# The first sixteen modulation units computed from rounded parts, in a fused two-block transformer kernel on one core

## The reference, cut to what matters

```python
c_act, cc_act = silu(c), silu(c_ctx)              # 1024 numbers each
mod   = c_act  @ ada_w[l] + ada_b[l]              # 1024 x 6144 for each layer l
mod_c = cc_act @ ada_w[l] + ada_b[l]
sh1, sc1, g1, sh2, sc2, g2 = split(mod, 6)
h  = x   * (1 + sc1)  + sh1                       # nothing else can start before this
hc = ctx * (1 + csc1) + csh1
```

## Time and profile before

| what | value |
|---|---|
| median of 3 runs | 2089.61 us (2089.19 to 2090.86) |
| the profiled execution | 2090.49 us, of which the span of its instructions is 2088.7 us |
| busy share of TensorE, VectorE, ScalarE, GpSimd | 93%, 58%, 44%, 52% |
| mean granted TensorE clock over the span | 0.966 of 2.4 GHz |
| HBM read | 342.68 MB, 165 GB/s over the span |
| first projection matmul starts | 46.41 us after the span's start |

### The profile page before, as it was taken

The page is one execution under the profiler, slowest core; times in us unless marked ns, Lnnn a source line. Parts: engine busy times, 40 slices in busy tenths (PEclk is TensorE's granted clock), DMA queues, the critical chain, the costliest instruction groups (busy, mean ns, idle before and its releaser), DMA issues.

```text
span 2088.7 us, 32983 instructions
## 1 busy us (share of the span) xinstructions
PE 1947.9 (93%) x11578; PEld 1617.5 (77%) x11578; DVE 1201.9 (58%) x2445; ACT 928.5 (44%) x1441; POOL 1082.7 (52%) x451
## 2 busy tenths in 40 slices
PE   7999888789979889969998989999999999999998
PEld 2644343589969779959777769999999998888887
DVE  1122645364455465450365231999999986777776
ACT  2212555445444445445524244654444445445553
POOL 0434556554439554427734047887666664444443
PEclk9998889799999999989999999999999999999999
DMA  8535465445545445535422335554444445555554
GB/s 288 172 131 171 151 217 181 139 159 182 190 141 181 159 150 185 189 112 195 162 88 83 120 121 179 184 181 152 145 150 147 147 148 191 194 192 191 192 194 156
DMA packets 95134, 345.08 MB, mean 165 GB/s; under 512 B 10512, under 2 KB 11840, under 8 KB 94528
## 3 DMA queue, kind: packets, MB, share of 16 engines
q1 hardware_dynamic: 90720, 329.82, 47.8%
q10 hardware_dynamic: 4320, 13.97, 2.0%
HBM read 342.68 MB, written 1.06 MB: 165 GB/s over the span
## 4 chain that ended last, share of the span: by engine, by line
PE 52%; issue 16%; DVE 14%; POOL 12%; DMA 3%; ACT 2%; ACTq 0%; POOLq 0%; SPq 0%; DVEq 0%
PE ps L505 18%; PE ps L458 16%; POOL ring_lo L403 10%; PE ps L442 4%; PE ps L649 3%; DMA ring<-stream 3%; PE ps L574 2%; PE ps L758 2%; DVE hot_hi_a L2279 1%; PE ps L720 1%; DVE hot_hi_b L2279 1%; DVE hot_lo_b L2280 1%; DVE hot_lo_a L2280 1%; DVE arena L1624 1%; DVE arena L2290 1%
## 5 line engine op out<-in xcount | busy, mean ns | idle before, releaser
L403 POOL TENSOR_TENSOR ring_lo<-ring,ring_hi 128x1024 fp32r<-128x1024 f32 x435 | 1047.2, 2412 | 993.5 <-ACT ring_hi L397 992.7
L397 ACT ACTIVATE ring_hi<-ring 128x1024 fp32r<-128x1024 f32 x580 | 613.4, 1058 | 573.3 <-DMA ring<-stream 570.1
L458 PE MATMUL ps<-h_lo,ring_hi 128*128 128x256 f32 x2096 | 295.9, 284 | 0.0
L458 PEld LDWEIGHTS ps<-h_lo,ring_hi 128*128 128x128 f32 x2096 | 272.2, 193 | 0.0
L505 PE MATMUL ps<-ring_hi,e_pair 128*128 128x512 f32 x1024 | 255.9, 391 | 2.6 <-DVE e_pair L2314 2.2
L2314 DVE TENSOR_TENSOR e_pair<-arena,e_pair 128x256 fp32r<-128x256 f32 x128 | 174.5, 1363 | 99.1 <-ACT e_pair L1477 99.1
L505 PEld LDWEIGHTS ps<-ring_hi,e_pair 128*128 128x128 f32 x1024 | 193.0, 189 | 43.8 <-DVE e_pair L2314 3.0
L403 DVE TENSOR_TENSOR ring_lo<-ring,ring_hi 128x1024 fp32r<-128x1024 f32 x145 | 191.9, 1324 | 5.0 <-ACT ring_hi L397 3.2
L505 PE MATMUL ps<-ring_hi,arena_r 128*128 128x512 f32 x704 | 186.2, 399 | 1.2 <-ACT ring_hi L397 1.2
L458 PE MATMUL ps<-late_r,ring_hi 128*128 128x256 f32 x1136 | 162.6, 286 | 0.0
L1980 DVE CAST arena_r<-arena 128x256 fp32r<-128x256 f32 x64 | 62.3, 974 | 169.5 <-ACT arena L1359 169.5
(11 more groups left out here) (278 smaller groups left out, 2463.1 us busy)
## 6 DMA issues: line engine op xcount, KB each, us to landing
ring<-stream SPq DMA_DIRECT2D x628, 512.0 KB, 3.3
arena<-ln_rows ACTq DMA_DIRECT2D x8, 512.0 KB, 5.8
arena<-ada_rows ACTq DMA_DIRECT2D x4, 512.0 KB, 4.6
arena<-decay ACTq DMA_DIRECT2D x1, 1536.0 KB, 7.2
cst<-consts ACTq DMA_DIRECT2D x1, 1036.0 KB
h<-x_t ACTq DMA_DIRECT2D x1, 1024.0 KB
arena<-ctx_t ACTq DMA_DIRECT2D x1, 1024.0 KB
late<-bias_rows ACTq DMA_DIRECT2D x1, 1024.0 KB, 7.9
```

Of the source, the lines that this page charges most:

```text
L397: act.activation(ring_hi[:, s, :], ring[:, s, :], ACT.Copy).then_inc(hi_ready, 1)
L403: eng.tensor_tensor(ring_lo[:, s, :], ring[:, s, :], ring_hi[:, s, :], ALU.subtract).then_inc(lo_ready[s], 1)
L458: m = pe.matmul(ps[:, bank, 0:T], w[:, kc * P:(kc + 1) * P], x[:, kc, :], start=begin, stop=w is w_lo and kc == KC - 1)
```

## The change

Units 0 to 15 are split like all later modulation units. Their products are made with `cact4` (the rounded and the remaining part of silu(c), four columns) instead of `cact`: two products with the rounded unit and two with the rest. ScalarE rounds each of the sixteen units; DVE subtracts for the even ones and POOL for the odd ones. ScalarE issues only the parameters first. The constants and the four small inputs are issued behind the rounding of unit 0 (`consts_in`, `rows_in`), the tokens behind that of unit 4, the context behind that of unit 6 (`inputs`, now counted to 2). ScalarE copies row g out behind the rounding of the last unit of row g+1, and the exp of the two lambda sums moves behind the sixteen roundings. On DVE the lambda work moves behind the first four subtractions. `bias_row` goes through bank 2 instead of 7 and stands before the last `early_columns`; DVE works on its result before the last `mod_columns`. POOL's eight subtractions stand in front of those of the later units.

```diff
-SPLIT_STAGES = (*(f"ada_mid{_n}" ...
+SPLIT_STAGES = ("ada0", *(f"ada_mid{_n}" ...
-                one(7, relb[0:32, 0:8], oneh[0:32, :], ps[0:8, 7, 0:DIST])
+                one(2, relb[0:32, 0:8], oneh[0:32, :], ps[0:8, 2, 0:DIST])
-            pe.wait_ge(cact_ready, 1)
+            pe.wait_ge(cact4_ready, 1)
             def early_rows(g):
-                    w = unit(FIRST_UNIT["ada0"] + 4 * g + k4)
-                    for k2 in range(2):
-                        kc = 2 * k4 + k2
-                        m = pe.matmul(ps[0:2, b, :], cact[:, kc, :], w[:, k2 * 512:(k2 + 1) * 512],
+                    u = FIRST_UNIT["ada0"] + 4 * g + k4
+                    w_hi, w_lo = split_unit(u)
+                    for w in (w_hi, w_lo):
+                        if w is w_lo:
+                            wait_unit_lo(u)
+                        for k2 in range(2):
+                            kc = 2 * k4 + k2
+                            m = pe.matmul(ps[0:4, b, :], cact4[:, kc, :], w[:, k2 * 512:(k2 + 1) * 512],
...
             for g in range(EARLY_ADA // 4):
                 early_rows(g)
                 if g == 0:
-                    pe.wait_ge(inputs, 16 * 7)
+                    pe.wait_ge(consts_in, 16)
                 else:
                     early_columns(g - 1)
+            pe.wait_ge(rows_in, 16 * 4)
+            bias_row()
             early_columns(EARLY_ADA // 4 - 1)
-            bias_row()
...
# ScalarE
-            for dst, src in ((relb[0:32, :], rel_bias), ..., (cst[:, :], consts), (h[:, :, :], x_t), (z, ctx_t)):
-                act.dma_start(dst, src).then_inc(inputs, 16)
...
+            for k in range(EARLY_ADA):
+                unit_hi(act, FIRST_UNIT["ada0"] + k)
+                if k == 0:
+                    act.dma_start(cst[:, :], consts).then_inc(consts_in, 16)
+                    for dst, src in ((relb[0:32, :], rel_bias), (oneh[0:32, :], onehot), (dmask[0:8, :], dist_mask),
+                                     (lamb, lam_in)):
+                        act.dma_start(dst, src).then_inc(rows_in, 16)
+                if k == 4:
+                    act.dma_start(h[:, :, :], x_t).then_inc(inputs, 16)
+                if k == 6:
+                    act.dma_start(z, ctx_t).then_inc(inputs, 16)
+                if k % 4 == 3 and k > 4:
+                    early_row_out(k // 4 - 1)
+            act.wait_ge(lam_sum, 1)
+            act.activation(lam2, lam2, ACT.Exp).then_inc(act_step, 1)
+            early_row_out(EARLY_ADA // 4 - 1)
# VectorE
+            dve.wait_ge(cact_hi, 1)
+            dve.tensor_tensor(cact4[:, :, 2:4], cact[:, :, :], cact4[:, :, 0:2], ALU.subtract).then_inc(cact4_ready, 1)
+            for k in range(0, 8, 2):
+                unit_lo(dve, FIRST_UNIT["ada0"] + k)
+            dve.wait_ge(rows_in, 16 * 4)
...
             for g in range(EARLY_ADA // 4):
+                if g < 2:
+                    for k in (8 + 4 * g, 10 + 4 * g):
+                        unit_lo(dve, FIRST_UNIT["ada0"] + k)
+                if g == 3:
+                    filled(2)
+                    step(dve.tensor_copy(rowbuf[0:8, :], ps[0:8, 2, 0:DIST]))
...
                 mod_columns(0, 6 + g % 2, 4 * g)
# GpSimd
+            for k in range(1, EARLY_ADA, 2):
+                unit_lo(pool, FIRST_UNIT["ada0"] + k)
```

More of the change, by code:

```diff
@@ L86 @@
 PROJ_UNIT = [FIRST_UNIT[f"proj{_n}"] for _n in range(N_PROJ)]
-SPLIT_STAGES = (*(f"ada_mid{_n}" for _n in range(N_PROJ)), "ada_late", "attn_out", "mlp0", "conv_in", "conv_out", "mlp1",
+SPLIT_STAGES = ("ada0", *(f"ada_mid{_n}" for _n in range(N_PROJ)), "ada_late", "attn_out", "mlp0", "conv_in", "conv_out", "mlp1",
                 "in2_qk", "in2_v", "in2_gates", "out2", "peer_q", "peer_u", "peer_v")
@@ L333, in build @@
         params_in = sem("params_in")
+        consts_in = sem("consts_in")
+        rows_in = sem("rows_in")
         inputs = sem("inputs")
@@ L587, in early_rows @@
                 for k4 in range(4):
-                    w = unit(FIRST_UNIT["ada0"] + 4 * g + k4)
-                    for k2 in range(2):
-                        kc = 2 * k4 + k2
-                        m = pe.matmul(ps[0:2, b, :], cact[:, kc, :], w[:, k2 * 512:(k2 + 1) * 512],
-                                      start=kc == 0, stop=kc == KC - 1)
-                        if k2 == 0:
-                            m.then_inc(units_begun, 1)
+                    u = FIRST_UNIT["ada0"] + 4 * g + k4
[6 more added lines that the diff above has]
+                            m = pe.matmul(ps[0:4, b, :], cact4[:, kc, :], w[:, k2 * 512:(k2 + 1) * 512],
+                                          start=w is w_hi and kc == 0, stop=w is w_lo and kc == KC - 1)
+                            if w is w_hi and k2 == 0:
+                                m.then_inc(units_begun, 1)
                 m.then_inc(full[b], 1)
@@ L603, in early_columns @@
                 for q in range(4):
-                    m = pe.matmul(ps[:, b, 2 * q:2 * q + 2], early_row[0:2, g, q * P:(q + 1) * P],
-                                  const("ident")[0:2, 0:2], start=True, stop=True)
+                    m = pe.matmul(ps[:, b, 2 * q:2 * q + 2], early_row[0:4, g, q * P:(q + 1) * P],
+                                  const("pair", 2)[0:4, :], start=True, stop=True)
                 m.then_inc(full[b], 1)
@@ L795, in _ @@
             pe.wait_ge(h_act, 1)
-            pe.wait_ge(cact4_ready, 1)
             projections()
@@ L1136, in _ @@
             act.dma_start(par[:, :], params).then_inc(params_in, 16)
-            for dst, src in ((relb[0:32, :], rel_bias), (oneh[0:32, :], onehot), (dmask[0:8, :], dist_mask),
-                             (lamb, lam_in), (cst[:, :], consts), (h[:, :, :], x_t), (z, ctx_t)):
-                act.dma_start(dst, src).then_inc(inputs, 16)
             act.wait_ge(params_in, 16)
@@ L1144, in _ @@
             act.activation(cact4[:, :, 0:2], cact[:, :, :], ACT.Copy).then_inc(cact_hi, 1)
-            act.wait_ge(lam_sum, 1)
-            act.activation(lam2, lam2, ACT.Exp).then_inc(act_step, 1)
             def drain(b, dst, func=ACT.Copy, n=T, **kw):
@@ L1150, in drain, with early_row_out @@
                 act.activation(dst, ps[:, b, 0:n], func, **kw).then_inc(emptied[b], 1)
-            for g in range(EARLY_ADA // 4):
+            def early_row_out(g):
                 act.wait_ge(full[EARLY_BANKS[g]], 1)
-                act.activation(early_row[0:2, g, :], ps[0:2, EARLY_BANKS[g], :], ACT.Copy).then_inc(
+                act.activation(early_row[0:4, g, :], ps[0:4, EARLY_BANKS[g], :], ACT.Copy).then_inc(
                     emptied[EARLY_BANKS[g]], 1)
+            for k in range(EARLY_ADA):
[14 more added lines that the diff above has]
+            early_row_out(EARLY_ADA // 4 - 1)
             drains[4].add()
@@ L1169, in _ @@
             act.wait_ge(mod_cols, 1)
+            act.wait_ge(inputs, 16 * 2)
             for c, src in enumerate((h, z)):
@@ L1526, in _ @@
             n_rstd = Count()
-            dve.wait_ge(params_in, 16)
-            dve.wait_ge(inputs, 16 * 7)
+            dve.wait_ge(cact_hi, 1)
[3 more added lines that the diff above has]
+            dve.wait_ge(rows_in, 16 * 4)
             step(dve.tensor_tensor(lamw, lamb[:, 0:4:2, :], lamb[:, 1:4:2, :], ALU.mult))
@@ L1536, in _ @@
             step(dve.tensor_scalar(mqg, param("mq_g"), SCALE, None, ALU.mult))
[L1537 to L1543, removed]
             def mod_columns(l, bank, at):
@@ L1552, in _ @@
             for g in range(EARLY_ADA // 4):
-                mod_columns(0, 6 + g % 2, 4 * g)
+                if g < 2:
[4 more added lines that the diff above has]
+                    step(dve.tensor_copy(rowbuf[0:8, :], ps[0:8, 2, 0:DIST]))
+                    settle()
+                    dve.tensor_tensor(rowbuf[0:8, :], rowbuf[0:8, :], dmask[0:8, :], ALU.add).then_inc(row_ready, 1)
+                    dve.wait_ge(row_ready, 1)
+                    dve.sem_inc(emptied[2], 1)
+                mod_columns(0, 6 + g % 2, 4 * g)
+            dve.wait_ge(act_step, 1)
+            step(dve.tensor_tensor(nlam, lam2[:, 1:2], lam2[:, 0:1], ALU.subtract))
+            settle()
+            step(dve.tensor_scalar(nlam, nlam, -LAM_INIT, None, ALU.add))
+            dve.wait_ge(inputs, 16 * 2)
             reads[0].add()
@@ L1590, in _ @@
                 m.then_inc(h_dve, 1)
[L1591 to L1596, removed]
             def rope(b, zs, n, cos, sin):
```

## The result

The changed kernel takes 2100.09 us (median of 6 runs, 2096.79 to 2102.10) against 2090.24 us for the kernel before (6 runs on the same chip, 2088.64 to 2092.58): a ratio of 1.0039 with a 95% interval of 1.0026 to 1.0052, so 9.9 us slower, where +3.4 was forecast and 2088.0 to 2097.3 given as the range.

What follows compares the result with a forecast made beforehand. TensorE, busy 93% of the span, was taken as the bound, with the opening's waits counted in full. First projection 49.0 + 0.8 for the clock = 49.8 against 46.4, +3.4, so 2093.0 us; range 2088.0 to 2097.3.

Steps and rivals of the forecast that it cites:

- a loop of load, rounding, POOL and products: Rows of the opening: waits from one load's issue round to the next make a row 8.6 us, against 8.2 before.
- the make-up of row 0: Opening, row 0: DVE and POOL subtract one after the other, DVE taking 2.56 instead of 1.22; row ends at 16.3.
- the landings of rows 2 and 3: Stream loads in rows 2 and 3 land 3.3 us after issue, with 4.3 kept for the range.
- the bias row's place in the tail: Before the last columns: bias row 0.8, then copy and addition 1.2; 3.0 before `mod_columns` against 1.9, +1.1.
- row 1: Opening: load 7 issued at 16.6, landed 21.9, rounded 23.0, subtracted 25.4; row ends at 25.9.
- tail: From the last products to the first projection: 5.6 us, against 4.5 before.
- first projection: End of the opening: starts at 43.4 + 5.6 = 49.0 us before the clock's share, against 46.4.
- an earlier end of row 0 would lower the sum by 0.2 us only: Row 0 would end at 15.2 without the lock; later rows are set by loads, so only 0.2 us is gained.
- I add 2.0 to the landing (5.3): Row 1, load 7: tokens and context passing nearby add 2.0 us to 3.3, between nothing and 4.1.
- I take 0.8: Opening rows: clock at 1.2 GHz throughout would cost 0.6 us a row, 1.8 in all; 0.8 was taken.
- Rival A: Opening: 1.2 GHz through all rows (+1.8), loads of 4.3 in rows 2 and 3 (+2.0); 2096.0 us; chance 0.22.
- Rival C: Behind the opening: the clock's pattern shifts, +-4 us around the forecast, 2089 or 2097; chance 0.13.

Runs made afterwards that it cites:

- e5: Changed kernel plus three unread float32 products in the wait for POOL's rest of each odd unit and three before the first projection: 2095.12 us, 1.0016.
- e7: Changed kernel with all sixteen subtractions on VectorE instead of every other one on POOL: 2093.98 us, ratio 1.0017 to the kernel before.
- e9: Changed kernel with all sixteen subtractions on VectorE, bias row behind the last columns, its VectorE work behind the modulation, and few fillers: 2092.80 us, 1.0017.
- e4: Changed kernel with the bias row behind the last columns and VectorE's work on it behind the modulation: 2096.50 us, ratio 1.0028.
- e11: Control: the changed kernel once more, unedited, for a second profile: 2102.16 us (one run), first projection at 55.98.
- e1: Changed kernel with tokens and context issued behind the rounding of unit 15 instead of units 4 and 6: 2098.57 us, ratio 1.0043.
- e2: Kernel before with the later order of loads alone, all products in float32, no split units: 2093.23 us, ratio 1.0011 (0.9994 to 1.0029).
- e6: Changed kernel with all seven inputs issued at the very start, as before the change, units still split: 2098.42 us, ratio 1.0041.
- e8: Changed kernel with tokens and context issued in eight pieces of 256 KB, behind the roundings of units 2 to 9: 2099.46 us, ratio 1.0040.
- e10: Control: the kernel before once more, unedited, for a second profile: 2093.36 us (one run), first projection at 48.32.
- e3: Changed kernel with unread float32 products filling TensorE's idle time before units, products with the rest and the first projection: 2106.28 us, ratio 1.0079.

## Why the prediction was wrong

The direction and the mechanism held: a loop of load, rounding, POOL and products sets the row, longer than a row in float32, though TensorE has less to do. So did the make-up of row 0 (DVE's second subtraction took 2.54 us behind POOL's, like 2.56 in the earlier trace rows), the landings of rows 2 and 3 (3.27 and 3.37 for 3.3), and the bias row's place in the tail (+1.1 forecast; at the full clock 5.8 in e5 and e7 with it and 4.6 in e9 without). The size did not: 49.0 was worked out before the clock's share, 56.15 came.

| term | forecast at 2.4 GHz | measured | difference |
|---|---|---|---|
| row 0 ends | 16.3 | 15.1 | -1.2 |
| row 1 | 9.6 | 13.4 | +3.8 |
| row 2 | 8.9 | 10.0 | +1.1 |
| row 3 | 8.6 | 10.0 | +1.4 |
| tail | 5.6 | 7.7 | +2.1 |
| first projection | 49.0 | 56.15 | +7.2 |

*Row 0* came 1.2 us early because the first of ScalarE's issues ran beside the rounding of unit 0: the next rounding began at 7.78 and not at 8.9. This was carried on. Load 7 was issued at 15.67 instead of 16.6, so the remark that an earlier end of row 0 would lower the sum by 0.2 us only does not agree with the prediction's own chain.

*The step "I add 2.0 to the landing (5.3)".* Load 7 took 8.2: +2.9 (7.1 in e4 and e11: +1.8). The earlier trace rows had the right size (7.39 at 10.87), and I took a middle between it and nothing because tokens and context were to pass one after the other. No row stood behind that middle. The order was much as forecast: the tokens were issued 1.8 us ahead of load 7 (forecast about 1.6), the context at 22.88 (forecast 20). The 1 MB of the tokens alone cost as much as I had seen for both. e1 shows the price, 3.0 to 4.2 us for having them in row 1, and e2, e6 and e8 that it is paid wherever they pass.

*The step "I take 0.8" for the clock.* This is the larger error. I had 0.6 us a row for 1.2 GHz, which is too little even by the earlier trace rows: three of a unit's four products at 1.87 instead of 0.92 for the four are 0.7 us more, before any columns. In the trace the columns have most of it. Eight short records take 0.98 us at one level and 1.79 at the other, the first product 0.34 and 0.53, while the second pair came at nearly the full pace (0.64 and 0.63): 1.0 us a row. e5, with the clock held, gives 8.9 for row 3 against 10.0. And I had given the tail nothing: two sets of columns and the bias row (1.37 against 0.75) make it 1.9 longer (7.7 against 5.8 in e5), though that hides VectorE's copy and addition. Row 1 has 0.4 (1.02 for a pair that takes 0.62). Together that is some 4.3 us where 0.8 stood. Rival A named this cause with +1.8, too small as well, and its loads of 4.3 us in rows 2 and 3 did not come. What is left of the table's differences is small, some tenths of a us a row: e5's row 3 is 8.9 at the full clock, where I had added up 8.6.

I read the clock of the opening before (1.00) as one that would mostly last. The runs show that it was not safe even in float32. Ahead of row 1 TensorE stood 3.41 us without products in the first profile, and the clock stayed at 1.00; in e10 it stood 2.03 us and the clock was 0.63 behind it; in e2, behind the load of 8.87 us, it was 0.50. In the rows after that the kernel before and e10 had 1.00 again (24 to 34 us, TensorE busy 9.8 us of 10). The change takes that dense work away, and e5, which puts work into the waits, has 1.00 there. The Trainium skill, "TensorE: Matmul & The Clock Gate", section "HAM oscillation", describes such a kernel, with groups of matmuls between waits for a DMA and the clock falling in them; by that rule the trace agrees, 0.50 over 24 to 34 us, behind 3.49 us without products. Which waits bring it down is not settled. Over 36 to 38 us, in the wait for POOL, it was 1.00, and in e4, whose work is the same up to there, it fell at 16 to 17 us (0.82, then 0.50) behind waits of at most 1.43 us.

*Rival C.* Behind the opening the spans of single executions differ by -6 to +4.5 us from the shift of the first projection, with no pattern that follows the edits. The medians follow that shift within 3.5 us in all nine experiments (the widest is e3, +18.4 there and +15.0 in the total), but all nine fall short of it, by 0.5 to 3.5 us. With e10's 48.32 as the start of the kernel before they lie within 1.6 us on both sides, so 46.41 may be an early example of it. That it is the clock which scatters behind the opening was not tried and stays open.

## What to carry to other kernels

A cheaper product makes a stretch longer when its operand must first pass two more engines and the ring ahead is short (three loads here; no run tried a deeper ring): add up one round from the load's issue to the next issue and compare it with what the engine took before. If the change takes work from TensorE in a stretch that was dense, price everything on its chain there at 1.2 GHz as one bound, the short records too, and look at more than one profile for the clock: it came out either way here for the same work. Bytes that are moved to another time are paid where the stream's loads are waited for.

## What the runs showed of the hardware that I had not expected

ScalarE issued a DMA that stands behind an activation in its program as that activation began (both at 13.86 us), and one (5.43) even ahead of the start of the rounding it stands behind (5.55). The four issues after it still held up the next rounding, until 7.78. A load of 512 KB that took 3.3 us apart from others took 8.2 us beside 1 MB on the other queue, which had all of the data for 2 us; 2 MB took 12.3 us beside three such loads. Behind the wait ahead of row 1 in the kernel before, the granted clock was 1.00 in one execution (3.41 us without products) and 0.63 in another (2.03 us). A few float32 products that nobody reads, three in TensorE's wait for the rest of each odd unit, went with a clock of 1.00 over 28 to 48 us, where the changed kernel had 0.50 to 1.00, and made rows with more work shorter.
